# SwiGLU up phases in an fp32 kernel of four residual blocks: 512-column products into pairs of PSUM banks

## The reference, cut to what matters

```python
def swiglu(h, w_gate_up, w_down):
    gu = h @ w_gate_up
    g, u = jnp.split(gu, 2, axis=-1)
    return (jax.nn.silu(g) * u) @ w_down    # 2816 -> 1024

for l in range(2):
    h = swiglu(rms_norm_2(x, ffn1_pre[l]), ffn1_w_gate_up[l], ffn1_w_down[l])
    x = x + 0.5 * rms_norm_2(h, ffn1_post[l])
    h = hybrid_mixer(rms_norm_2(x, mix_pre[l]), ...)
    x = x + rms_norm_2(h, mix_post[l])
    h = swiglu(rms_norm_2(x, ffn2_pre[l]), ffn2_w_gate_up[l], ffn2_w_down[l])
    x = x + 0.5 * rms_norm_2(h, ffn2_post[l])
```

## Time and profile before

| | |
|---|---|
| median of 3 runs | 1967.78 us (1967.46 to 1968.02) |
| the profiled execution | 1967.11 us |
| its span, first to last instruction | 1965.3 us |
| granted TensorE clock, mean over the span | 0.970 of full |
| TensorE busy, VectorE, ScalarE, GpSimd | 96%, 69%, 48%, 7% of the span |
| weights rounded on ScalarE (L213) | 313 x 1.914 us |
| rests on VectorE (L222) | 313 x 2.296 us |

### The profile page before, as it was taken

One profiled execution on the slowest core, in us unless ns is written; L12 is line 12 of the kernel. 1 busy time (PEld: TensorE's weight loads), 2 busy tenths in 40 slices (PEclk: granted clock), 3 DMA queues, 4 the chain that ended last, 5 costly groups with the idle time before them and its releaser, 6 DMA issues.

```text
span 1965.3 us, 34117 instructions
## 1 busy us (share of the span) xinstructions
PE 1884.1 (96%) x14532; PEld 1825.0 (93%) x14532; DVE 1351.2 (69%) x1676; ACT 937.6 (48%) x1101; POOL 134.5 (7%) x119
## 2 busy tenths in 40 slices
PE   7969999988999999999999999999999999999997
PEld 7938999988999899989999999989998999999997
DVE  5797898566799656666785666656665686576664
ACT  5443665446666444444354454435443444354442
POOL 0000333000132100000300000000000030000000
PEclk9968999998999999999999989999999999989999
DMA  7312555533455534554455445554555445445451
GB/s 283 141 43 76 179 197 185 201 119 129 172 196 191 199 142 175 192 193 156 168 199 188 172 150 178 189 212 145 177 190 205 144 177 191 166 150 193 179 206 67
DMA packets 46797, 334.82 MB, mean 170 GB/s; under 512 B 5184, under 2 KB 5568, under 8 KB 6464
## 3 DMA queue, kind: packets, MB, share of 16 engines
q1 hardware_dynamic: 46512, 332.20, 47.0%
q0 software_dynamic: 144, 0.52, 0.1%
HBM read 331.65 MB, written 1.05 MB: 169 GB/s over the span
## 4 chain that ended last, share of the span: by engine, by line
PE 89%; DVE 7%; ACT 2%; issue 1%; DMA 1%; SPq 0%; DVEq 0%; ACTq 0%
PE psum L240 20%; PE psum L241 19%; PE psum L242 19%; PE psum L255 10%; PE psum L277 8%; PE psum L258 5%; PE psum L284 3%; DVE w_lo L222 2%; PE psum L316 1%; DVE scratch L1262 1%; PE psum L483 1%; PE psum L486 1%; PE psum L485 1%; PE psum L338 1%; DMA w_raw<-stream_in 0%
## 5 line engine op out<-in xcount | busy, mean ns | idle before, releaser
L213 ACT ACTIVATE w_hi<-w_raw 128x2048 fp32r<-128x2048 f32 x313 | 598.1, 1914 | 764.9 <-PE psum L242 457.9
L240 PE MATMUL psum<-x_split,w_hi 128*128 128x256 f32 x2984 | 848.1, 284 | 11.0 <-DVE x_split L354 10.4
L241 PE MATMUL psum<-x_split,w_hi 128*128 128x256 f32 x2984 | 845.1, 283 | 0.0
L242 PE MATMUL psum<-x_split,w_lo 128*128 128x256 f32 x2984 | 845.0, 283 | 0.0
L222 DVE TENSOR_TENSOR w_lo<-w_raw,w_hi 128x2048 fp32r<-128x2048 f32 x313 | 717.4, 2296 | 69.1 <-ACT w_hi L213 69.1
L240 PEld LDWEIGHTS psum<-x_split,w_hi 128*128 128x128 f32 x2984 | 573.5, 192 | 12.3 <-issue 11.2
L241 PEld LDWEIGHTS psum<-x_split,w_hi 128*128 128x128 f32 x2984 | 573.6, 192 | 0.1
L242 PEld LDWEIGHTS psum<-x_split,w_lo 128*128 128x128 f32 x2984 | 573.4, 192 | 0.0
L296 DVE TENSOR_TENSOR scratch<-psum,inv_rms 128x512 f32<-128x512 f32 (+1 forms) x205 | 139.5, 687 | 254.2 <-PE psum L242 238.7
L255 PE MATMUL psum<-h_split,w_hi 128*128 128x512 f32 x816 | 288.6, 399 | 0.0
L258 PE MATMUL psum<-h_split,w_lo 128*128 128x256 f32 x816 | 229.2, 281 | 0.0
(11 more groups left out here) (203 smaller groups left out, 1900.4 us busy)
## 6 DMA issues: line engine op xcount, KB each, us to landing
w_raw<-stream_in SPq DMA_DIRECT2D x313, 1024.0 KB, 4.8
x_resid<-x_in SPq DMA_DIRECT2D x1, 1024.0 KB, 6.9
y_out<-x_resid SPq DMA_DIRECT2D x4, 256.0 KB, 2.5
scratch<-mask_in SPq DMA_DIRECT2D x1, 768.0 KB, 11.0
scratch<-ev_in SPq DMA_DIRECT2D x1, 512.0 KB, 9.6
scratch<-inv_in POOLq DMA_DIRECT2D x1, 512.0 KB, 3.9
params<-par_in SPq DMA_DIRECT2D x1, 247.0 KB, 7.2
matrices<-mat_in SPq DMA_DIRECT2D x1, 192.0 KB, 9.0
```

What stands on the lines that cost most here:

```text
L213: act.activation(w_hi[:, n % RING, :], raw[:, n % RAWS, :], ACT.Copy).then_inc(hi_ready, 1)
L240: pe.matmul(dst, w_hi[:, c.slot, b:b + P], src[:, k0 + k, 0, :], start=opens, stop=False)
L241: pe.matmul(dst, w_hi[:, c.slot, b:b + P], src[:, k0 + k, 1, :], start=False, stop=False)
L242: done = pe.matmul(dst, w_lo[:, c.slot, b:b + P], src[:, k0 + k, 0, :], start=False, stop=last and k == nk - 1 and m == len(tiles_) - 1)
```

## The change

In upA and upB of both layers, chunks 3 to 21 (19 of 22) become wide. A wide chunk owns two events and two neighbouring banks, so an up phase has 2 x 22 - 3 = 41 events. TensorE multiplies it with `multiply_wide` (w_hi times 512 columns, w_lo times 256). ScalarE, ahead of rounding the next weights, copies the right halves of both banks into the ACC slots (one ACTIVATE, 128x512). VectorE waits for that copy, adds the left halves to it into scratch (which frees both banks), waits for its own add, and multiplies by the inverse rms in place. The gate's silu waits for the multiply instead of the take. TensorE waits for the last of the chunk's two events: `c.last + 1`. Chunks 0 to 2 stay as they are.

```diff
+NARROW = 3
+WIDE = ("upA", "upB")
@@
-LAYER = [("upA", FF2, FF2), ...
+LAYER = [("upA", FF2, 2 * FF2 - NARROW), ...
@@ class Chunk
+        self.wide = phase in WIDE and n >= NARROW
+        self.event = E0[phase] + n + layer * LAYER_EVENTS + (n - NARROW if self.wide else 0)
         self.bank = self.event % BANKS
+        self.last = self.event + 1 if self.wide else self.event
@@ multiply_wide(..., ready=None, hooks={})
-                pe.wait_ge(*ready(k0 + k))
+                if ready is not None:
+                    pe.wait_ge(*ready(k0 + k))
@@ take_scaled
             dve.wait_ge(chunk_done, c.number + 1)
+            if c.wide:
+                dve.wait_ge(up_right, wide_count(c))
+                dve.tensor_tensor(dst, ps[:, c.bank:c.bank + 2, 0:T], S(ACC + 2 * c.slot, 2),
+                                  ALU.add).then_inc(pair_taken, 2)
+                dve.wait_ge(*taken(c.last))
+                dve.tensor_tensor(dst, dst, rinv[:, :].unsqueeze(1).to_broadcast([P, 2, T]),
+                                  ALU.mult).then_inc(up_scaled, 1)
+                return
@@ pre_pe (chunk 2) and whole_pe
-                pe.wait_ge(pair_taken, c.event + 1)
+                pe.wait_ge(pair_taken, c.last + 1)
                 pe.wait_ge(lo_ready, c.number + 1)
-                multiply(pe, c, pair_tiles(c.bank), xs, 0, KT, True, True, signal=(chunk_done, 1))
+                whole(pe, c)
+        def whole(pe, c, hooks={}):
+            if c.wide:
+                multiply_wide(pe, c, (c.bank, c.bank + 1), xs, 0, KT, True, True, hooks=hooks)
+            else:
+                multiply(pe, c, pair_tiles(c.bank), xs, 0, KT, True, True, signal=(chunk_done, 1), hooks=hooks)
@@ up_act
-                act.wait_ge(*(... else taken(c.event - prev)))
+                act.wait_ge(*(... else scaled(Chunk(phase, c.n - prev, l))))
@@
                 act.wait_ge(chunk_done, c.number + 1)
+                if c.wide:
+                    act.activation(S(ACC + 2 * c.slot, 2), ps[:, c.bank:c.bank + 2, T:2 * T], ACT.Copy)\
+                       .then_inc(up_right, 1)
                 refill_hi(act, c)
```

More of the change, by code:

```diff
@@ L44 @@
          ("up1", FF1, FF1), ("down1", 12, 7)]
-LAYER = [("upA", FF2, FF2), ("downA", 12, 7), ("bg", 4, 4), ("pool_in", 4, 4), ("cv", 8, 8),
+LAYER = [("upA", FF2, 2 * FF2 - NARROW), ("downA", 12, 7), ("bg", 4, 4), ("pool_in", 4, 4), ("cv", 8, 8),
          ("gates", 8, 8), ("conv_out", 4, 4), ("pool", 1, 4), ("pool_out", 4, 4),
-         ("w_o", 4, 4), ("upB", FF2, FF2), ("downB", 12, 7)]
+         ("w_o", 4, 4), ("upB", FF2, 2 * FF2 - NARROW), ("downB", 12, 7)]
 C0, E0 = {}, {}
@@ L147, in __init__ @@
     def __init__(self, phase, n, layer=0):
-        self.n, self.buf = n, n % 3
+        self.n, self.buf, self.phase, self.layer = n, n % 3, phase, layer
         self.number = C0[phase] + n + layer * LAYER_CHUNKS
         self.slot = self.number % RING
-        self.event = E0[phase] + n + layer * LAYER_EVENTS
+        self.wide = phase in WIDE and n >= NARROW
+        self.event = E0[phase] + n + layer * LAYER_EVENTS + (n - NARROW if self.wide else 0)
         self.bank = self.event % BANKS
+        self.last = self.event + 1 if self.wide else self.event
 def chunks(phase, count, layer=0, done=0):
@@ L200, in program @@
         pair_taken = sem("psum_pair_taken")
+        up_scaled = sem("up_pair_scaled")
+        up_right = sem("up_right_halves_copied")
         const_landed = sem("const_landed")
@@ L247, in multiply, with multiply_wide @@
                 done.then_inc(*signal)
-        def multiply_wide(pe, c, banks, src, k0, nk, first, last, ready):
+        def multiply_wide(pe, c, banks, src, k0, nk, first, last, ready=None, hooks={}):
             for k in range(nk):
-                pe.wait_ge(*ready(k0 + k))
+                if ready is not None:
+                    pe.wait_ge(*ready(k0 + k))
                 for m, bank_ in enumerate(banks):
@@ L259, in multiply_wide @@
                                      start=False, stop=last and k == nk - 1)
+                if k in hooks:
+                    hooks[k]()
             done.then_inc(chunk_done, 1)
@@ L366, in pre_pe @@
                     c = Chunk(ph, 2, l)
-                    pe.wait_ge(pair_taken, c.event + 1)
+                    pe.wait_ge(pair_taken, c.last + 1)
                     pe.wait_ge(lo_ready, c.number + 1)
-                    multiply(pe, c, pair_tiles(c.bank), xs, 0, KT, True, True, signal=(chunk_done, 1),
-                             hooks={3: lambda: mean_pe(pe, tr, summed, l), 6: lambda: rinv_pe(pe, tr, l)})
+                    whole(pe, c, hooks={3: lambda: mean_pe(pe, tr, summed, l), 6: lambda: rinv_pe(pe, tr, l)})
                     done = 3
@@ L602, in up_tracks, with wide_count, scaled @@
             return {k: Signal(sem(f"{name}_{k}_ready"), 2 * m if k == "taps" else m) for k in names}
+        def wide_count(c):
+            return (WIDE.index(c.phase) + 2 * c.layer) * (FF2 - NARROW) + c.n - NARROW + 1
+        def scaled(c):
+            if c.wide:
+                return up_scaled, wide_count(c)
+            return taken(c.event)
         def up_act(act, phase, n, tr, func, conv, pre, l):
@@ L608, in gate @@
                 s = (c.slot - prev) % RING
-                act.wait_ge(*(tr["gate"].count(c.n + 1 - prev, l) if conv else taken(c.event - prev)))
+                act.wait_ge(*(tr["gate"].count(c.n + 1 - prev, l) if conv else scaled(Chunk(phase, c.n - prev, l))))
                 act.activation(S1(GEL + s), S1((ACC + 2 * s + 1) if conv else (PRE + 2 * s)), func)\
```

## The result

| | before | after |
|---|---|---|
| median, same chip and time | 1967.46 us (5 runs, 1966.84 to 1968.02) | 1956.02 us (5 runs, 1953.64 to 1958.37) |
| the profiled execution, span | 1967.11, 1965.3 | 1954.39, 1952.6 |

In this measurement single executions of the new kernel lie further apart (4.7 us) than those of the old one (1.2), though a later one of the old kernel spread over 8.9 us. Two later measurements of the same kernel gave 1958.56 and 1957.28; all 14 executions average 1957.2, and 43 of the kernel before 1967.5. So the gain is 10.3 us on average.

The account below looks back on a forecast made before the run. TensorE's matmul pitch was taken as the bound; 8.1 us saved in wide chunks less 3.2 lost at four heads gave -4.9 us, so a median of 1962.9 us (0.25% less), range 1959.6 to 1966.0.

Parts of the forecast that it names:

- The bound: In the up phases time is TensorE's pitch times its matmuls, 0.120 us per narrow one; the other engines wait.
- the covers: Up phases: ScalarE's and VectorE's added work costs nothing, VectorE's step becoming 4.97 us, under 5.653 by 0.68.
- The copy: ScalarE's 128x512 copy from PSUM for each wide chunk: 0.62 us, bounds 0.38 and 0.77, hidden.
- The stop at the heads: Chunk 3 waits for the take of chunk 0: 0.79 us lost at each of four heads, 3.2 us, bounds 2.0 and 4.0.
- A wide chunk of 16 pairs therefore takes 5.653 us instead of 5.760: 0.107 less: Up phases: the down phases' 0.3533 us a pair applied to 76 wide chunks, saving 8.1 us.
- (c): Rival: the wide form's pitch gains half or nothing in the up phases; time between 1963.8 and 1971.0 us, chance 0.24.
- The Trainium skill's gap rule: Joining two matmuls in wide chunks saves only 2.5 ns, 3.0 us in all, less than the heads' loss; put at 1968.0.

Follow-up runs that it names:

- restarts: The changed kernel with TensorE stopped ahead of each wide chunk from number 4 on and of each group of the down phases: 2118.07 us (one execution).

## Why the prediction was wrong, point by point

- **The bound** was right: TensorE's pitch times its matmuls. What was said of the covers held. The copy took 0.598 us (forecast 0.62), VectorE kept 0.7 us of slack, TensorE never waited for an add or for w_lo in the steady state, and the stages without a changed phase changed by no more than 1.4 us, less than the 2.5 between two profiles of the same kernel.
- **The stop at the heads** was right in place and cause. Start to start it lost 0.65 us (0.77 - 0.12), 0.75 with the slow first pair; the forecast was 0.79. Alone it cost 2.6 us for four, forecast 3.2 with bounds 2.0 and 4.0. The restart took 0.06 us after the take, not 0.20; the slow first pair makes up most of that difference.
- **The step that failed** is "A wide chunk of 16 pairs therefore takes 5.653 us instead of 5.760: 0.107 less". It was right for 8 of the 12 up phases profiled in the kernel's three profiles. In the other 4 a chunk took 5.547, 0.213 less, and the down phase behind it ran at that pitch too. I took the down phases' pitch as the form's own, since it stood the same in all six. But all six are entered from a running stream, and I had myself worked out that the change makes TensorE enter from rest. The sum thus lacked a term of -2.9 us for each stretch that catches the low pitch: -5.8 in the profiled execution, and on average -2.9 if one head in four catches it, -3.9 at the 4 of 12 seen.
- **The remainder.** 4.9 + 3.9 is 8.8 us, and 10.3 were measured in the mean of 14 executions. The changed stages at the high pitch gained 1.3 to 1.5 us each instead of 1.2, which makes 9.1 to 9.9. The last 0.4 to 1.2 us stays open. It is less than the up to 2.7 us by which other medians missed their forecasts, and that the 14 executions caught the low pitch as often as the three profiled ones isn't known.
- **The rivals.** None was it. (c) looked for a worse pitch than the down phases', and no rival for a better one. The Trainium skill's gap rule ("TensorE: Matmul & The Clock Gate", section "Back-to-back issue gap"), by which joining two matmuls returns 2.5 ns, lies further off than the prediction had it: 2 x 0.120 - 0.227 = 13 ns at the low pitch.

## What to carry to other kernels

A pitch read where a stream is entered one way holds for that way of entering: where a change makes the engine start from rest, or alternates two widths, leave room for another pitch on both sides. When a form alternates, try its order: putting the two 512-column matmuls of a k-block together and the two 256-column ones behind gave one steady pitch and 8 us more than the change itself, of which 4 to 6 come from the down phases that already had the wide form.

## What was not expected of the hardware

TensorE's stream of alternating 512- and 256-column matmuls ran at either 0.3467 or 0.3533 us a pair at a granted clock of 1.00. Which one was settled at a start from rest (25 of 94 starts at the low one, in `restarts`) and then held for up to 436 pairs, across chunks and phases. The low one repeats every two pairs (0.69 us), the high one every three (1.06 us). Entered from a stream of 256-column matmuls without a stop, it was 0.3533 in all 24 phases looked at. Two short matmuls joined save 13 ns at the low pitch and 6.7 at the high one.
